# Two sums over partitions as products of rounded operands, in a hybrid decoder step on one core

## What is computed

```python
def rms_norm(x, g):
    y = x * lax.rsqrt(jnp.mean(x * x, axis=-1, keepdims=True) + EPS)
    return y * g

xn = rms_norm(x, g_pre)                                   # the first norm
u_a, v_a, z_a, q_b, k_b, v_b, z_b, a_lr, m_a, m_b = split_cols(xn @ w_in)
...                                                       # spatial gating and gated linear attention
log_a = log_sigmoid(a_lr @ w_a2 + b_a) / GATE_TAU
m = sigmoid(m_a) * (y_a @ w_pa) + sigmoid(m_b) * (y_b @ w_pb)
h = x + rms_norm(m @ w_o, g_post)                         # the last norm
h = h + sigmoid(h @ w_pg) * (p @ w_pe)
```

## Time and profile before

| | us |
|---|---|
| median of 3 runs | 957.93 (957.87 to 958.04) |
| profiled execution | 957.94 |
| its span | 956.2 |
| TensorE busy with products | 950.7 |
| VectorE busy | 557.8 |
| ScalarE busy | 374.2 |
| GpSimd busy | 105.6 |

### The profile page before, as it was taken

The page is one execution under the profiler, slowest core; times in us unless marked ns, Lnnn a source line. Parts: engine busy times, 40 slices in busy tenths (PEclk is TensorE's granted clock), DMA queues, the critical chain, the costliest instruction groups (busy, mean ns, idle before and its releaser), DMA issues.

```text
span 956.2 us, 17383 instructions
## 1 busy us (share of the span) xinstructions
PE 950.7 (99%) x6666; PEld 941.1 (98%) x6666; DVE 557.8 (58%) x769; ACT 374.2 (39%) x467; POOL 105.6 (11%) x103
## 2 busy tenths in 40 slices
PE   9999999999999999999999999999999999999998
PEld 8999999999999999999999999999999999999998
DVE  6758778737796576444444444444455444696443
ACT  7445244232253444333333333333333333464331
POOL 0000001112243640000000000000002333100000
PEclk9999999999999999999999999999999999999999
DMA  9645435877654454444444444444447444336541
GB/s 348 215 134 177 145 125 181 241 236 247 223 172 140 160 168 141 155 154 153 141 147 152 154 141 151 147 153 154 151 143 270 154 153 146 119 135 223 175 155 39
DMA packets 56879, 160.47 MB, mean 168 GB/s; under 512 B 6532, under 2 KB 20616, under 8 KB 56840
## 3 DMA queue, kind: packets, MB, share of 16 engines
q1 hardware_dynamic: 42640, 143.18, 45.1%
q10 hardware_dynamic: 14200, 16.75, 5.3%
HBM read 150.56 MB, written 9.34 MB: 167 GB/s over the span
## 4 chain that ended last, share of the span: by engine, by line
PE 98%; DVE 1%; DMA 1%; ACT 0%; issue 0%; ACTq 0%; SPq 0%; DVEq 0%
PE bank L1259 29%; PE bank L1260 29%; PE bank L1261 29%; PE bank L1313 1%; PE bank L1526 1%; PE bank L1322 1%; PE bank L1316 1%; PE bank L1523 1%; PE bank L1529 1%; PE bank L1287 0%; PE bank L1286 0%; PE bank L1285 0%; PE bank L1470 0%; PE bank L1409 0%; DMA params<-in_params 0%; PE bank L1420 0%
## 5 line engine op out<-in xcount | busy, mean ns | idle before, releaser
L706 DVE TENSOR_TENSOR w_lo<-w_raw,w_hi 128x1024 fp32r<-128x1024 f32 x252 | 315.5, 1257 | 335.0 <-ACT w_hi L398 167.0
L1259 PE MATMUL bank<-x_hi,w_hi 128*128 128x320 f32 x1216 | 377.3, 310 | 0.0
L1261 PE MATMUL bank<-x_hi,w_lo 128*128 128x320 f32 x1216 | 375.7, 309 | 0.0
L1260 PE MATMUL bank<-x_lo,w_hi 128*128 128x320 f32 x1216 | 375.7, 309 | 0.0
L398 ACT ACTIVATE w_hi<-w_raw 128x1024 fp32r<-128x1024 f32 x148 | 155.8, 1058 | 262.7 <-PE bank L1261 238.7
L1259 PEld LDWEIGHTS bank<-x_hi,w_hi 128*128 128x128 f32 x1216 | 228.2, 188 | 2.5 <-issue 2.2
L1260 PEld LDWEIGHTS bank<-x_lo,w_hi 128*128 128x128 f32 x1216 | 228.3, 188 | 0.1
L1261 PEld LDWEIGHTS bank<-x_hi,w_lo 128*128 128x128 f32 x1216 | 228.2, 188 | 0.0
L603 ACT ACTIVATE w_hi<-w_raw 128x1024 fp32r<-128x1024 f32 x96 | 101.6, 1059 | 115.8 <-PE bank L1261 115.8
L1259 PE MATMUL bank<-m_hi,w_hi 128*128 128x320 f32 x448 | 138.4, 309 | 0.0
L1260 PE MATMUL bank<-m_lo,w_hi 128*128 128x320 f32 x448 | 138.4, 309 | 0.0
(11 more groups left out here) (233 smaller groups left out, 892.3 us busy)
## 6 DMA issues: line engine op xcount, KB each, us to landing
w_raw<-in_w_units SPq DMA_DIRECT2D x258, 512.0 KB, 3.3
state_dec<-in_s ACTq DMA_DIRECT2D x8, 512.0 KB, 6.2
out_st_dec<-state_dec ACTq DMA_DIRECT2D x8, 512.0 KB, 5.6
h<-in_x_t ACTq DMA_DIRECT2D x4, 640.0 KB, 6.5
out_y<-pe_out ACTq DMA_DIRECT2D x16, 160.0 KB, 2.1
x_sb<-in_x_t SPq DMA_DIRECT2D x6, 320.0 KB, 7.8
v_rows<-v_parts SPq DMA_DIRECT2D x4, 256.0 KB
v_stacked_rows<-v_rows SPq DMA_DIRECT2D x4, 256.0 KB, 7.0
```

The lines of the kernel that those rows point to most:

```text
L706: dve.tensor_tensor(wlo[:, q], raw[:, q], whi[:, q].bitcast(F32), ALU.subtract).then_inc(lo_ready, 1)
L1259: pe.matmul(acc, h, hi[:, k0 + k, :], start=first and k == 0, stop=False)
L1260: pe.matmul(acc, h, lo[:, k0 + k, :], start=False, stop=False)
L1261: m = pe.matmul(acc, l, hi[:, k0 + k, :], start=False, stop=last and k == UK - 1)
```

## The change

Both sums over partitions become two products of float32r operands. VectorE writes the last addition twice, once rounded to float32r (part 0) and once in full, waits for its own results and subtracts them to get part 1. TensorE multiplies both parts by a rounded copy of the ones, `ones_r`, which VectorE makes once, behind the first sum's parts; a semaphore `ones_set` is added. In the last norm the sum moves from ahead of tile 2 to ahead of tile 3 of group 0. The small area grows by 512 bytes a partition for `ones_r`.

```diff
@@ building the tiles
-        SMALL = 19 * KB + 256
+        SMALL = 19 * KB + 256 + 512
+        sq_parts = at("squares_parts", M0 + 2 * slot + 2 * TB, [P, 2, T], F32R)
+            if name == "tmp":
+                last_parts = at("last_squares_parts", off + 2 * TB, [P, 2, T], F32R)
+        ones_r = at("ones_r", off, [P, P], F32R)
@@ vector engine, first norm
-            dve.tensor_tensor(squares[:, 0, :], squares[:, 0, :], squares[:, 1, :], ALU.add).then_inc(sq_ready, 1)
+            def add_in_parts(parts, total, x, y):
+
+                own.up(dve.tensor_tensor(parts[:, 0, :], x, y, ALU.add))
+                then(dve.tensor_tensor(total, x, y, ALU.add))
+                return dve.tensor_tensor(parts[:, 1, :], total, parts[:, 0, :].bitcast(F32), ALU.subtract)
+
+            add_in_parts(sq_parts, squares[:, 4, :], squares[:, 0, :], squares[:, 1, :]).then_inc(sq_ready, 1)
             dve.wait_ge(consts_loaded, 16 * 5)
+            dve.tensor_copy(ones_r[:], ones).then_inc(ones_set, 1)
@@ vector engine, last norm
-                    dve.tensor_tensor(tmp[:, 1, :], tmp[:, 0, :], sig[:, 0, :], ALU.add).then_inc(sum_last, 1)
+                    add_in_parts(last_parts, tmp[:, 1, :], tmp[:, 0, :], sig[:, 0, :]).then_inc(sum_last, 1)
@@ tensor engine
+            def sum_parts(acc, parts):
+
+                pe.matmul(acc, ones_r[:], parts[:, 0, :], start=True, stop=False)
+                return pe.matmul(acc, ones_r[:], parts[:, 1, :], start=False, stop=True)
@@ tensor engine, first norm
             pe.wait_ge(sq_ready, 1)
-            pe.matmul(bank[5][:, 0:T], ones, squares[:, 0, :], start=True, stop=True).then_inc(sum_done, 1)
+            pe.wait_ge(ones_set, 1)
+            sum_parts(bank[5][:, 0:T], sq_parts).then_inc(sum_done, 1)
@@ tensor engine, last norm
-                    if n == 0 and c == 2:
+                    if n == 0 and c == 3:
 
                         pe.wait_ge(sum_last, 1)
-                        pe.matmul(bank[NORM_BANK][:, 0:T], ones, tmp[:, 1, :], start=True, stop=True)\
-                          .then_inc(sum_done, 1)
+                        sum_parts(bank[NORM_BANK][:, 0:T], last_parts).then_inc(sum_done, 1)
```

More of the change, by code:

```diff
@@ L250, in build @@
         alrw_ready = sem("alrw_ready")
+        ones_set = sem("ones_set")
         x_rounded, x_split = sem("x_rounded"), sem("x_split")
```

## The result

The changed kernel takes 959.32 us (median of 22 runs, 958.26 to 961.99) where the kernel before took 958.05 beside it (957.68 to 958.51): a ratio of 1.0013 with a 95% interval of 1.0007 to 1.0019, so 1.27 us more. By both it is slightly slower, within the 0.2% that was set as no change. The forecast was 959.41, 1.47 us more.

A forecast was written before the change was run, and what follows sets the result against it. TensorE, busy 950.7 of 956.2 us, was taken to bound the kernel. 957.94 + 0.90 (first norm) + 0.57 (last norm) = 959.41 us, 0.15% slower; range 958.4 to 960.3.

The forecast's parts named there:

- both waits for line 640: Last norm: TensorE would newly wait for ScalarE's bank-freeing copies, 0.5 us at 833 and some 0.3 us near 839.
- TensorE's wait for `a_lr_sum`: Before line 1340, after the first norm: this wait would grow from 0.3 to 1.4 us.
- Line 1340 doesn't move: Sign of a wrong prediction: TensorE's products with `w_a2` were to start at 52.58 instead of 51.68 us.
- the first norm's term: First sum: VectorE's added work delays the chain to TensorE's line 1340, +0.90 us; TensorE's saving there is worth nothing.
- the last norm's term: Last sum: line 720 0.64 us later delays line 640's copies and TensorE's line 1523, +0.57 us, 0.24 saving already deducted.
- the 0.90 us arrive in full: First norm: line 720's delay on VectorE passes undiminished through the chain to TensorE's line 1340, +0.90 us.
- No link has spare time: Chain from line 720 to line 1340: each link was released by the one before, so 0.90 us passes through.
- The copy of the ones: First norm, VectorE's queue: copying 128 columns was taken as 0.15 us, bounds 0.06 and 0.31.
- Covers at both sites: Rival: VectorE's extra work is free at both norms, TensorE saves 0.24 and gains 0.3 us, 957.40 us; chance 0.07.
- only site one costing: Rival: only the first norm costs, TensorE keeps its 0.24 us at the last norm, 958.60 us; chance 0.14.
- The products are cheaper: Opposing rival: the rounded pair costs 0.53 us, line 720 another 0.24 later at the last norm, 959.65 us; chance 0.05.
- The store didn't collide: Rival: first norm's store of `a_rows` meets the weight loads' tail and slows by 0.8 us, 960.21 us; chance 0.14.

The follow-up runs named there:

- change again: The changed kernel unedited, measured and profiled a second time against the kernel before: 958.71 against 958.02 us, +0.69.
- first alone: Only the first norm's sum changed, last norm as in the kernel before: 958.33 against 957.91 us, +0.42.
- VectorE's work only: First norm's edit on VectorE only, TensorE still multiplying in full precision, against the kernel before: 958.71 against 958.02 us, +0.69.
- more work: First norm's edit plus two more VectorE additions into tiles nobody reads, against the kernel before: 958.55 against 958.02 us, +0.53.
- last alone: Only the last norm's sum changed, at tile 3, first norm as in the kernel before: 958.59 against 957.91 us, +0.68.
- last, tile 2: Only the last norm's sum changed, kept ahead of tile 2 as in the kernel before: 958.31 us, +0.40.
- last, copies first: Only the last norm's sum changed, ScalarE copying group 0 ahead of the root and group 2 ahead of h's fourth tile: 957.89 against 957.94 us before.
- late `w_a2` products: Kernels taking `w_a2` products one q step later: first norm's sum changed 957.52; kernel before, copies first 957.59; whole change, copies first 957.24, also group 1 957.11 us.
- first comparison: The changed kernel's first measurement beside the kernel before: 959.32 against 958.05 us, ratio 1.0013.
- the run that takes the wait away: Only the first norm's sum changed, TensorE taking the products with `w_a2` one q step later: 957.52 against 957.94 us before, -0.42.
- variance first: Only the first norm's sum changed, VectorE norming `a_lr` before splitting units 10 and 11: 963.09 us, +5.18 against the kernel before.

## Why the prediction held

**The signs that it named.** Not all of them came. Line 720's like started at 38.32 and 38.39 in the two profiles (38.5 forecast), and both waits for line 640 are there. But TensorE's wait for `a_lr_sum` was 0.6 and 1.6 us (1.4), the store took 2.16 and 3.28 us (2.9), and line 1340's like started at 51.60 and 52.81 (52.6). "Line 1340 doesn't move" was named as a sign of being wrong, and in the first profile it didn't move. In that execution the first norm's term was nothing; the forecast holds as a median over executions, not in each.

**What the first norm costs in one execution.** The profiles can be added up. From the start of the parts' loads to line 1340 are 51.68 - 44.30 = 7.38 us before. TensorE comes there 16.91 us after its start of line 1300 (51.37 - 34.46) with the full-precision sum and 16.66 with the rounded one (51.25 - 34.59), and needs 0.2 us for the change of operands even without a wait. The later of the two, plus 957.94 - 51.68 = 906.26, plus the last norm's term, should be the profiled time:

| profile | chain | TensorE | last norm | sum | measured |
|---|---|---|---|---|---|
| before | 51.68 | 51.57 | 0 | 957.94 | 957.94 |
| change | 51.61 | 51.17 | 0.57 | 958.44 | 958.37 |
| change again | 52.81 | 51.45 | 0.57 | 959.64 | 959.58 |
| first alone | 51.69 | 51.32 | 0 | 957.95 | 957.94 |
| VectorE's work only | 52.77 | 51.28 | 0 | 959.03 | 959.02 |
| more work | 52.65 | 51.22 | 0 | 958.91 | 958.91 |
| last alone | 51.04 | 52.08 | 0.57 | 958.91 | 958.86 |
| last, tile 2 | 51.27 | 51.83 | 0.33 | 958.42 | 958.44 |
| last, copies first | 51.53 | 51.52 | -0.04 | 957.75 | 957.77 |

The last norm's terms are the forecast ones, and for the copies first the 0.24 saved less the 0.2 waited. All nine agree within 0.07 us (the first by construction, since the constants are taken from it). So the places and the mechanism were right, and what varies is visible: in the four profiles with the old first norm the later of the two is 51.53 to 52.08 us, mean 51.78; in the four that have the new first norm and no added work it is 51.61 to 52.81, mean 52.22. That is +0.44, which the run of the first norm alone showed (+0.42). Four more profiles can be read up to the parts' loads, those of the kernels with late `w_a2` products, which differ only behind them. With these there are five with the old first norm and seven with the new one, and the means are 51.79 and 52.35: +0.56. The ranges overlap, so this size is an estimate too.

**The term that was mis-sized** is "the 0.90 us arrive in full". VectorE's delay was 0.89, and it did reach the end of the chain: on average the parts' loads start at 43.99 us in the five profiles with the old first norm and at 44.97 in the seven with the new one. What took a part of it up was TensorE. By the table's rule it comes to line 1340 at 51.77 us on average in the five, 0.4 us behind the chain's own mean of 51.37 (43.99 + 7.38): in three of them it is the later of the two, by 0.5 to 1.0 us. The profile of before caught it at the early end of its start-up: line 1300 started 34.46 us into the span there and 34.41 to 34.97 in the others of this kind. Where TensorE starts later, the sum also comes later and VectorE waits for it (0.39 to 0.62 us in the same three). "No link has spare time" was read from one execution in which the chain was last by 0.11 us; over several executions it is not. The cost was 0.42 and 0.69 us by the two runs that have it alone (the second without TensorE's saving); as the whole change less the last norm alone it is 0.59 in the first comparison and 0.01 in the second, so its size is known to some 0.3 us only, and that it is above zero rests on the profiles and on the run that takes the wait away (0.84 less).

**The last norm's term** was 0.57 and its run gave 0.68. Both waits for line 640 stood where they were forecast (0.45 us for 0.5, and 0.37 for some 0.3 over the third and fourth loads of line 1523), and taking their cause away took the time away.

**The copy of the ones** cost 0.13 of VectorE's queue for 0.15. The wait between additions and subtraction cost what it was given: the subtraction started 0.04 us after its producer's end, against 0.08 before the end without a wait.

**The rivals.** Covers at both sites, and only site one costing, fall to the run of the last norm alone. The products are cheaper: 0.25 us apart at 36.61 and 36.86 and then 0.15 to the next product, 0.40 at the first norm and 0.29 at the last. The store didn't collide as that rival put it, by 0.8 us on top of 2.94; it took 1.8 to 3.3 us in all profiles here. That its length matters was right, and both signs occur. That the forecast came within 0.2 us of the first comparison is luck in part: the first norm's term was 0.2 to 0.5 too high, the last norm's 0.1 too low, and against the second comparison (0.69 more instead of 1.47) the forecast is twice the measured change.

**What stays open.** In all profiles but that of the variance first, thirteen, the store landed 0.2 to 1.0 us behind the last of the four weight loads, however early it was issued; in nine of them it was 0.41 to 0.45 us, with the store issued anywhere from 41.29 to 42.44. It landed at 44.28 behind 43.86 before, at 45.41 behind 44.49 in the second profile of the change, at 43.64 behind 42.64 in the run of the last norm alone. On average the last weight load lands 0.99 us later with the new first norm (44.45 for 43.46) and the parts' loads start 0.98 later, though the store is issued only 0.55 later (42.09 for 41.54). That would make the splits, and not line 720, the chain's true link here, since they release these loads. It is an observation beside which no run was made that moves one without the other; in the one that moved both the store took 2.3 us and landed ahead of a weight load issued behind it (43.49, where that one landed at 45.87), and the cost was of another kind. What made one execution of the change take 961.99 us is open as well: its mean granted clock was 0.998, as in the run with the variance first, but it has no profile. Nor is it known what sets the start of line 1300.

## What to carry to other kernels

An engine that the profile's page shows at 58% can be on the path of the one at 99%: look, behind each operation that is added, for the queue up to the next thing that somebody else waits for, and compare its spare time with the added time. Where a step is moved to avoid a wait, ask who is released by its end; the wait may be cheaper. And a spare time of a tenth of a microsecond read from one execution is a draw from a range. More profiles of the kernel before would have shown it here: the chain was last by 0.11 us in the first one, and TensorE by 0.5 to 1.0 us in three of the four other profiles with the old first norm.

## What the runs showed of the hardware

Four loads of 160 KB took 2.6 to 3.4 us with no weight load beside them and 5.5 to 8.1 with four of 512 KB under way (the run with the variance first). In the same run TensorE waited 3.1 us, and its granted clock then fell to 0.50, the 1.2 GHz level, for about 3.5 us; this cost some 1.5 us on top of the 2.7 that the products started later. Waits of up to 1.7 us in the other profiles left the clock at 1.00. A full-precision product with 320 columns cost TensorE 0.53 us of its stream and two rounded ones 0.29. Starts of the same line differed by up to 0.8 us between executions of like kernels (34.17 to 34.97 for line 1300).
